# Twelve Strassen row tile pairs in the down projection, with all their sums on DVE

## What is computed

```python
  u = RMSNorm(x) @ W_up
  x  += W_down( silu(conv3(u)_gate) * conv3(u)_val )
  x  += sigmoid(RMSNorm(x) @ W_pg) * (p[i] @ W_ple)
```

## Time and profile before

| | |
|---|---|
| median of 3 runs | 1438.44 us (1438.39 to 1438.5) |
| the profiled execution's own time | 1438.39 us |
| its span | 1436.6 us |
| PE busy | 1425.5 us, 99% of the span |
| DVE busy | 985.1 us, 69% |
| ACT busy | 760.0 us, 53% |
| POOL busy | 216.9 us, 15% |
| granted TensorE clock | 0.999 |

### The profile page before, as it was taken

How to read it: one execution, slowest core, us unless ns; L and a number is a source line. 1 busy time by engine, 2 the same in 40 slices (tenths; PEclk the granted TensorE clock), 3 DMA queues, 4 the chain that set the end, 5 groups by cost and what they waited for, 6 DMA issues and landing times.

```text
span 1436.6 us, 19705 instructions
## 1 busy us (share of the span) xinstructions
PE 1425.5 (99%) x7112; PEld 1212.1 (84%) x7112; DVE 985.1 (69%) x1180; ACT 760.0 (53%) x920; POOL 216.9 (15%) x153
## 2 busy tenths in 40 slices
PE   9999999999999999999999999999999999999997
PEld 7888888888888888888888888888888888888886
DVE  7576777845455455566777777777777887787755
ACT  7555655544444444555555555555555546554544
POOL 0044144100000000000101101111011531140000
PEclk9999999999999999999999999999999999999999
DMA  9765555456666655465666566565665656565653
GB/s 325 225 205 161 165 176 159 143 194 190 191 190 191 191 190 188 158 208 181 190 188 191 180 198 186 179 204 175 191 193 177 212 192 200 177 213 188 227 200 121
DMA packets 190875, 273.47 MB, mean 190 GB/s; under 512 B 11744, under 2 KB 103136, under 8 KB 190688
## 3 DMA queue, kind: packets, MB, share of 16 engines
q1 hardware_dynamic: 190384, 272.30, 59.6%
q10 hardware_dynamic: 432, 0.37, 0.1%
HBM read 270.53 MB, written 2.10 MB: 190 GB/s over the span
## 4 chain that ended last, share of the span: by engine, by line
PE 98%; DVE 1%; issue 1%; ACT 0%; ACTq 0%; POOLq 0%; POOL 0%; DVEq 0%
PE main L622 15%; PE main L624 15%; PE main L623 15%; PE aux L747 11%; PE main L747 11%; PE aux L756 6%; PE main L756 6%; PE main L672 3%; PE main L670 3%; PE main L671 3%; PE aux L670 3%; PE aux L672 3%; PE aux L671 3%; PE aux L788 1%; PE aux L818 1%
## 5 line engine op out<-in xcount | busy, mean ns | idle before, releaser
L1301 DVE TENSOR_TENSOR w_lo<-raw,w_hi 128x1024 fp32r<-128x1024 f32 (+1 forms) x490 | 612.4, 1260 | 394.5 <-ACT w_hi L1009 394.3
L1009 ACT ACTIVATE w_hi<-raw 128x1024 fp32r<-128x1024 f32 (+1 forms) x490 | 514.1, 1052 | 541.2 <-PE main L624 284.8
L622 PE MATMUL main<-w_hi,xT 128*128 128x512 f32 x702 | 276.8, 394 | 0.0
L624 PE MATMUL main<-w_hi,xT 128*128 128x512 f32 x702 | 273.6, 390 | 0.0
L623 PE MATMUL main<-w_lo,xT 128*128 128x512 f32 x702 | 273.6, 390 | 0.0
L747 PE MATMUL aux<-xT,w_hi 128*128 128x512 f32 x704 | 169.9, 391 | 0.0
L747 PE MATMUL main<-xT,w_hi 128*128 128x512 f32 x672 | 163.0, 391 | 0.0
L624 PEld LDWEIGHTS main<-w_hi,xT 128*128 128x128 f32 x702 | 131.9, 188 | 27.4
L622 PEld LDWEIGHTS main<-w_hi,xT 128*128 128x128 f32 x702 | 132.0, 188 | 27.0 <-issue 0.4
L623 PEld LDWEIGHTS main<-w_lo,xT 128*128 128x128 f32 x702 | 132.0, 188 | 26.1
L747 PEld LDWEIGHTS aux<-xT,w_hi 128*128 128x128 f32 x704 | 129.4, 188 | 25.2 <-issue 0.3
(11 more groups left out here) (270 smaller groups left out, 1770.7 us busy)
## 6 DMA issues: line engine op xcount, KB each, us to landing
raw<-in_w_up SPq DMA_DIRECT2D x336, 256.0 KB
raw<-in_w_in SPq DMA_DIRECT2D x136, 512.0 KB
raw<-in_w_down SPq DMA_DIRECT2D x84, 512.0 KB
raw<-in_w_out SPq DMA_DIRECT2D x32, 512.0 KB
raw<-in_w_ple_gate SPq DMA_DIRECT2D x32, 512.0 KB
raw<-in_w_branch_a SPq DMA_DIRECT2D x16, 512.0 KB
raw<-in_w_branch_b SPq DMA_DIRECT2D x16, 512.0 KB
raw<-in_w_in SPq DMA_DIRECT2D x15, 256.0 KB, 5.7
```

The source lines that it names most:

```text
L622: pe.matmul(acc, th, wh, start=first, stop=False)
L624: return pe.matmul(acc, tl, wh, start=False, stop=end)
L1009: ac.activation(w_hi[:, u % RING, :, 0:w], raw[:, u % RING, :, 0:w], ACT.Copy).then_inc(hi_full, 1)
L1301: dve.tensor_tensor(w_lo[:, u % RING, :, 0:w], raw[:, u % RING, :, 0:w], w_hi[:, u % RING, :, 0:w].bitcast(F32), ALU.subtract).then_inc(lo ...
```

## The change

Per half, six pairs instead of five are made in Strassen's scheme, now alternately two and three pairs apart (it was three throughout). The activation sums move from POOL to DVE, in slot U - 3, ahead of the weight sums (slot U - 2, as before). Their rounded copies get two buffers, and ACT rounds them one slot earlier. POOL has no work left in the down projection. The transposes of the second `obT` stand two units later, and the four of the new x one unit later, as do the splits that read them.

```diff
-OBT = [PV[g] + 4 for g in range(2)]
+OBT = [PV[g] + 4 + 2 * g for g in range(2)]
-SEVEN_AT = ((5, 8, 11, 14, 17), (5, 8, 11, 14, 17))
+SEVEN_AT = ((5, 7, 10, 12, 15, 17), (5, 7, 10, 12, 15, 17))
-X2_AT = {down_slot(n) + 1: n for n in range(NQ)}
+X2_AT = {down_slot(n) + 2: n for n in range(NQ)}
...
-        a_sums_hi = sb("a_sums_hi", [P, 4, P], F32R, ffn)
-        a_sums_lo = sb("a_sums_lo", [P, 4, P], F32R, ffn)
+        a_sums_hi = sb("a_sums_hi", [P, 2, 4, P], F32R, ffn)
+        a_sums_lo = sb("a_sums_lo", [P, 2, 4, P], F32R, ffn)
...
-                    sp.wait_ge(w_summed, 3 * (SEVEN[u - RING] + 1))
+                    sp.wait_ge(w_summed, 2 * (SEVEN[u - RING] + 1))
...
                 if part == 0:
                     ac.wait_ge(a_summed, q + 1)
-                    if q:
-                        ac.wait_ge(w_sums_done, 2 * q)
+                    if q > 1:
+                        ac.wait_ge(w_sums_done, 2 * (q - 1))
...
+                if s + 2 in SEVEN:
+                    sums_hi(SEVEN[s + 2], 0)
                 if s + 1 in SEVEN:
-                    sums_hi(SEVEN[s + 1], 0)
                     sums_hi(SEVEN[s + 1], 1)
                 if s in SEVEN:
                     sums_hi(SEVEN[s], 2)
...
-            def weight_sums(u):
+            def weight_diffs(u):
 
                 q, a, b = SEVEN[u], u % RING, u % RING + 1
-                dve.tensor_tensor(w_sums[:, 0:2, :], raw[:, b, 0:2, :], raw[:, a:b + 1, 0, :], ALU.subtract).then_inc(w_summed, 1)
-                dve.wait_ge(w_summed, 3 * q + 1)
+                if q:
+                    dve.wait_ge(w_sums_ready, 2 * q)
+                dve.tensor_tensor(w_sums[:, 0:2, :], raw[:, b, 0:2, :], raw[:, a:b + 1, 0, :], ALU.subtract).then_inc(w_diffs, 1)
+                dve.wait_ge(w_diffs, q + 1)
...
+            def act_sums(u, q):
+
+                k = u - DOWN - 2 * UD * (u >= DOWN + 2 * UD)
+                if q:
+                    dve.wait_ge(a_sums_ready, q)
+                dve.tensor_tensor(a_sums[:], aT_hi[:, k:k + 2, :].bitcast(F32), aT_lo[:, k:k + 2, :].bitcast(F32),
+                                  ALU.add).then_inc(a_joined, 1)
+                dve.wait_ge(a_joined, q + 1)
+                a = a_sums[:].rearrange("p k (b t) -> p k b t", t=P)
+                a11, a12, a21, a22 = a[:, 0, 0], a[:, 1, 0], a[:, 0, 1], a[:, 1, 1]
+                dve.tensor_tensor(a22, a21, a22, ALU.add).then_inc(a_sum_part, 1)
+                dve.wait_ge(a_sum_part, 3 * q + 1)
+                dve.tensor_tensor(a21, a11, a21, ALU.subtract).then_inc(a_sum_part, 1)
...
+                if s + 3 in SEVEN:
+                    act_sums(s + 3, SEVEN[s + 3])
                 if s + 2 in SEVEN:
-                    weight_sums(s + 2)
+                    weight_diffs(s + 2)
                 if s + 1 in SEVEN:
                     sums_lo(SEVEN[s + 1], 0)
...
-                        if s == at + 2:
+                        if s == at + 1 + norm:
                             lo_blocks(name, xT_lo, xT_hi, 4 * n, VCOL[vec] + 4 * n, xT_hi_ready, xT_ready, 4 * (NQ * norm + n))
...
-            for q, u in enumerate(SEVENS):
-                act_sums(u, q)
             root(2)
```

More of the change, by code:

```diff
@@ L355, in build @@
             sem, ("pT_hi_ready", "pT_ready", "sig_ready", "emb_ready", "y_pre"))
[L357 to L360, removed]
+        w_diffs, w_summed, w_sums_hi_ready, w_sums_ready, w_sums_done = map(
+            sem, ("w_diffs", "w_summed", "w_sums_hi_ready", "w_sums_ready", "w_sums_done"))
+        a_joined, a_sum_part, a_summed, a_sums_hi_ready, a_sums_ready = map(
+            sem, ("a_joined", "a_sum_part", "a_summed", "a_sums_hi_ready", "a_sums_ready"))
         x2_turned, copied, combined = map(sem, ("x2_turned", "copied", "combined"))
@@ L675, in act_block, with act_sum @@
                 return aT_hi[:, k, tb * P:(tb + 1) * P], aT_lo[:, k, tb * P:(tb + 1) * P]
-            def act_sum(k):
-                return a_sums_hi[:, k, :], a_sums_lo[:, k, :]
+            def act_sum(q, k):
+                return a_sums_hi[:, q % 2, k, :], a_sums_lo[:, q % 2, k, :]
             def ring_tile(u, t):
@@ L710, in down_seven @@
                     pe.wait_ge(a_sums_ready, q + 1)
-                    mm = triple(down_acc(2 * p + 1, 0), *act_sum(2), *ring_tile(u, 1), start=False, stop=False)
+                    mm = triple(down_acc(2 * p + 1, 0), *act_sum(q, 2), *ring_tile(u, 1), start=False, stop=False)
                 mm.then_inc(units_done, 1)
@@ L719, in down_sums @@
                 if half == 0:
-                    triple(product(p, 1), *act_sum(3), *sum_tile(0), start=first, stop=end)
-                    mm = triple(product(p, 3), *act_sum(1), *sum_tile(1), start=first, stop=end)
+                    triple(product(p, 1), *act_sum(q, 3), *sum_tile(0), start=first, stop=end)
+                    mm = triple(product(p, 3), *act_sum(q, 1), *sum_tile(1), start=first, stop=end)
                 else:
-                    triple(product(p, 2), *act_sum(0), *sum_tile(2), start=first, stop=end)
+                    triple(product(p, 2), *act_sum(q, 0), *sum_tile(2), start=first, stop=end)
                     mm = triple(down_acc(2 * p, 1), *act_block(2 * i + 1, 1), *sum_tile(3), start=False, stop=False)
@@ L1154, in sums_hi @@
                     ac.wait_ge(a_summed, q + 1)
-                    if q:
-                        ac.wait_ge(w_sums_done, 2 * q)
-                    ac.activation(a_sums_hi[:].rearrange("p k t -> p (k t)"), a_sums[:].rearrange("p k t -> p (k t)"),
+                    if q > 1:
+                        ac.wait_ge(w_sums_done, 2 * (q - 1))
+                    ac.activation(a_sums_hi[:, q % 2].rearrange("p k t -> p (k t)"), a_sums[:].rearrange("p k t -> p (k t)"),
                                   ACT.Copy).then_inc(a_sums_hi_ready, 1)
@@ L1160, in sums_hi @@
                     half = part - 1
-                    ac.wait_ge(w_summed, 3 * q + (1, 3)[half])
+                    ac.wait_ge(w_summed if half else w_diffs, 2 * (q + 1) if half else q + 1)
                     if q:
@@ L1539, in up_post @@
                     dve.tensor_tensor(aT_lo[:, k, :], act[:, 0:nf, :], aT_hi[:, k, :].bitcast(F32), ALU.subtract).then_inc(aT_ready, 1)
-            def weight_sums(u):
+            def weight_diffs(u):
                 q, a, b = SEVEN[u], u % RING, u % RING + 1
-                dve.tensor_tensor(w_sums[:, 0:2, :], raw[:, b, 0:2, :], raw[:, a:b + 1, 0, :], ALU.subtract).then_inc(w_summed, 1)
-                dve.wait_ge(w_summed, 3 * q + 1)
+                if q:
+                    dve.wait_ge(w_sums_ready, 2 * q)
+                dve.tensor_tensor(w_sums[:, 0:2, :], raw[:, b, 0:2, :], raw[:, a:b + 1, 0, :], ALU.subtract).then_inc(w_diffs, 1)
+                dve.wait_ge(w_diffs, q + 1)
                 dve.tensor_tensor(w_sums[:, 2, :], raw[:, b, 1, :], w_sums[:, 0, :], ALU.subtract).then_inc(w_summed, 1)
-                dve.wait_ge(w_summed, 3 * q + 2)
+                dve.wait_ge(w_summed, 2 * q + 1)
                 dve.tensor_tensor(w_sums[:, 3, :], raw[:, a, 1, :], w_sums[:, 2, :], ALU.subtract).then_inc(w_summed, 1)
+            def act_sums(u, q):
[10 more added lines that the diff above has]
+                dve.tensor_tensor(a21, a11, a21, ALU.subtract).then_inc(a_sum_part, 1)
+                dve.wait_ge(a_sum_part, 3 * q + 2)
+                dve.tensor_tensor(a11, a22, a11, ALU.subtract).then_inc(a_sum_part, 1)
+                dve.wait_ge(a_sum_part, 3 * q + 3)
+                dve.tensor_tensor(a12, a12, a11, ALU.subtract).then_inc(a_summed, 1)
             def sums_lo(q, part):
@@ L1553, in sums_lo @@
                     dve.wait_ge(a_sums_hi_ready, q + 1)
-                    dve.tensor_tensor(a_sums_lo[:].rearrange("p k t -> p (k t)"), a_sums[:].rearrange("p k t -> p (k t)"),
-                                      a_sums_hi[:].rearrange("p k t -> p (k t)").bitcast(F32), ALU.subtract).then_inc(a_sums_ready, 1)
+                    dve.tensor_tensor(a_sums_lo[:, q % 2].rearrange("p k t -> p (k t)"), a_sums[:].rearrange("p k t -> p (k t)"),
+                                      a_sums_hi[:, q % 2].rearrange("p k t -> p (k t)").bitcast(F32), ALU.subtract).then_inc(a_sums_ready, 1)
                 else:
@@ L1814, in _ @@
                 pool.tensor_tensor(dec[:, 0, :], dec[:, 0, :], g_tok[:].rearrange("p b n -> p (b n)"), ALU.mult).then_inc(o_gated, 1)
[L1816 to L1835, removed]
             def product(j, nf, it=None):
```

## The result

The changed kernel takes 1450.99 us (median of 6 runs, 1448.23 to 1453.05) against 1438.41 us before in the same runs: a ratio of 1.0087, 95% interval 1.0076 to 1.0098. 1448.6 had been forecast. The profiled execution is the slowest of the six (1453.05 us, mean granted clock 0.995); the fastest, 1448.23 us, has a mean clock of 0.999 and the other four have 0.996. The profile's span is 1451.2 us, 14.6 more than before.

A forecast was written before the change was run, and what follows sets the result against it. PE was taken to bound the kernel. From 1438.39 us, fewer matmuls and removed waits took 3.76 and new stalls behind DVE's added work gave 14.0: 1448.6 us, 8-in-10 range 1440.5 to 1454.5.

The forecast's parts named there:

- the mean: Down projection, over five pairs: DVE needs 25.1 us and PE 25.8, so the load fits by 3%.
- the short gaps: Strassen pairs two pairs apart, three per half: PE waits 2.2 us each for activation sums, 14.0 us with weight-sum waits.

The follow-up runs named there:

- one short gap per half: Changed kernel with Strassen pairs at 5, 8, 11, 14, 16 in both halves, ten pairs with only the last two two apart: 1439.68 us.

## What to carry to other kernels

Where a bound engine is fed by others, compare the loads over each short stretch that the buffers can't bridge, and not the mean: 25.1 us of DVE work per 25.8 us of PE looked enough, and 11.4 per 10.2 in the short gaps cost 12 us of stalls. Price a saved matmul by the distance between starts (0.23 us), not by its shown duration (0.39), before work is loaded on a feeding engine for it: here 7.4 us of DVE work bought 0.68 us of PE. And separate the parts of a bundled change: moving some transposes by a unit or two gained 2.4 us, and the rest lost six times as much.

## What the hardware showed beyond that

Stalls of PE of 2.15 us in an otherwise full stream were followed in three of four cases by a fall of the granted clock to 0.50, 1.4 us after PE had resumed at the first of them, with PE busy all that time; the one stall of 2.17 us in the profile with one short gap per half was not. Behind stalls of 1.41 us and less no profile here has a fall while PE has work. What decides it between the two sizes, and why one in four escaped, no run shows. POOL's additions beside DVE lengthened DVE's operations of two SBUF inputs from 1.22 to 1.48 us; the Trainium skill ("SBUF — State Buffer", section "Who interferes with whom") says that a DVE instruction with two SBUF inputs contends with a GpSimd instruction that reads SBUF. The direction agrees; the size in this trace is 0.26 us per operation, though POOL's own last 1.3 us each.
